# Cross-attention laid into the query projection, weights released by halves, first loads reordered, and the router's first tile moved before the second tile's turn

## The chip, the cores and the metric

One core of one Trainium2 chip. The metric is the device time of one execution in microseconds; for the kernel before it is the median of three runs. The five engines named below are PE (TensorE, matmuls and transposes), DVE (VectorE), ACT (ScalarE), POOL (GpSimd) and SP (which here only issues transfers). Each works through its own list of instructions in order and waits on semaphores.

## What is computed

A two-layer transformer block followed by one mixture-of-experts block, on 256 rows of width 1024 in float32. What the change touches, cut down:

```
# block 1, each of 2 layers: mixer, then cross-attention, then SwiGLU, each followed by a layer norm
q = (u @ cq_w).reshape(B, S, 4, 256)
k, v = split(mem @ ckv_w)
p = softmax(einsum('bshd,bmhd->bhsm', q, k) * 256 ** -0.5)
o = einsum('bhsm,bmhd->bshd', p, v).reshape(B, S, 1024)
cross = o @ co_w
# block 2: after attention and the merge
x = x + g_a * (y @ w_out)
hf = rms(x) * (1 + sc_f) + sh_f
# router: 4 groups of 4 experts, best group, best two experts of it
x = x + g_f * moe(hf)
```

## The kernel before, in words

All weights are streamed once, as units of 1 MB (128 partitions of 2048 floats), in the order that `stream_plan` writes out. A unit lands in one of three raw buffers (five in the expert stage, where two "landing" buffers join). `split_half` turns each half of it (1024 columns) into a high part `whs` by an ACT copy (L207) and a low part `wls` by a DVE subtraction (L211); there are three such split slots, and in the last stage a fourth. Every product is done as three matmuls on those parts (`mm3`, L199). A unit's raw buffer is free for the next transfer when its second half is split; its split slot is free when the last matmul that reads it is done. Up to three units are split ahead. `release` (a unit's last matmul) puts as many splits into the lists of ACT and DVE as there are free slots (`pump`), unless `state["hold"]` or `state["slow"]` is set; with `slow` the splits come one half at a time at each `tick`; `feed(k)` puts in k halves at once. So the splits stand in the same ordered lists as all other work of ACT and DVE.

`gemm_fm` multiplies with the weights as the stationary side (two units, four column tiles of four steps each, two banks) and `gemm_tm` with the activations stationary (two units, two row tiles t). Before the change every matmul of a unit waits for both halves (`split_tok[n]` is a flat list of the two tokens). Both call `tick()` along the way, and a tick advances the first generator in `side`, which is how small chains (transposes, softmaxes) are laid between weight matmuls. `finish_side()` runs what is left.

First loads (L407 on): identity, condition vector, then the two row tiles of x, then the weights, all on SP's list. The two tiles are transposed (`to_fm`, L203), split into high and low parts by ACT and DVE, and the first units are split behind them.

Cross-attention (`cross`): both halves of the query projection `cq_w` run first (`gemm_fm`, four units), and `q_evac` copies each bank out, even ones by ACT, odd ones by DVE (L225). Then `attend` runs with no weight matmuls beside it: `scores(t, hp)` for row tile t and head pair hp (PE; then DVE maximum L222 and scaling L215, ACT exponentials L208, DVE reciprocal L228 and two scalings L215); `turn(hd)` transposes the probabilities of a head (L203; copied out by ACT or DVE); `weigh(hd)` multiplies by the values (L199; high part by ACT, low part by DVE L211). Only then does the output projection `co_w` begin.

The router's surroundings: `w_out_2` is multiplied in two column halves; `merge_evac` adds to the residual h and, with the second half, normalises a row tile (the reciprocal root by POOL, L231). In the middle of the last matmul group `f_fm(0, True)` transposes row tile 0, with all eight modulations on ACT. Behind the projection come, in this order: the low parts of tile 0 (DVE), `f_fm(1)` (transposes of tile 1, modulations, high and low parts), the table `count`, `feed(2)`, `router(0)` (24 small matmuls, logits copied by ACT), `turn_rows(0)` (16 transposes, four ACT copies), `router(1)`. A chain of small DVE operations then chooses experts and places (`first`, `second` are places of a row's two copies), the flag is written, all engines read it and branch, and in the branch `gather` builds the one-hot matrices `Pall` on DVE and multiplies the rows by them (32 matmuls, each bank's four in a row). The expert stage follows.

## Time and profile before

| what | value |
|---|---|
| median of three runs | 1680.62 us (1676.35 to 1683.83) |
| the profiled execution | 1681.34 us |
| its span in the profile | 1679.4 us |
| PE busy in the span | 1596.6 us (95%) |
| DVE, ACT, POOL busy | 1151.0, 903.9, 79.7 us |

The profile is of one execution. A row of its timeline gives the start, the duration, engine, line of the kernel, operation, written tile <- read tiles, shape, count, and in brackets how long the engine had been idle and what released it. The span is 1.94 us shorter than the time of that execution; sums are made against 1681.34.

### The profile page before, as it was taken

To read this page: it belongs to the slowest core of one execution; us is meant where nothing else is said; L and a number is where in the kernel's file an instruction comes from. 1 tells how busy PE (TensorE), PEld (TensorE's weight loads), DVE (VectorE), ACT (ScalarE), POOL (GpSimd) and SP (SyncE) were. 2 spreads that over 40 slices of the span, in tenths; PEclk is the share of its full clock that TensorE was granted. 3 is DMA by queue.
4 is the path that set the end of the run, shared out by engine and by line. 5 is a ranking of instruction groups with operands and counts; after the bars stand their busy time and mean duration, and the time that the engine had idled before them with its cause. 6 is when DMAs were issued, how large, how long until landed. Compare 5 with 4: busy or idle time off the path is not lost.

```text
span 1679.4 us, 20455 instructions
## 1 busy us (share of the span) xinstructions
PE 1596.6 (95%) x8036; PEld 1303.4 (78%) x8036; DVE 1151.0 (69%) x1617; ACT 903.9 (54%) x1377; POOL 79.7 (5%) x75
## 2 busy tenths in 40 slices
PE   7999999989999999989999899999989969999997
PEld 7987788776888789878878667888767758777786
DVE  7457655657545584667566478866664669999997
ACT  5466443435444364764434254544353448888885
POOL 0010000001000000100000000000200000000005
PEclk9999999999999999999999999999999879999999
DMA  7445234535654454542356278874440318999995
GB/s 286 177 153 198 89 112 158 194 126 211 242 198 177 149 202 175 204 172 86 116 200 226 75 259 296 315 257 175 150 169 26 119 63 302 364 374 369 370 371 177
DMA packets 52202, 339.35 MB, mean 202 GB/s; under 512 B 7835, under 2 KB 8477, under 8 KB 13316
## 3 DMA queue, kind: packets, MB, share of 16 engines
q1 hardware_dynamic: 48932, 331.79, 53.7%
q0 software_dynamic: 3168, 6.20, 1.0%
q8 instruction: 65, 1.06, 0.3%
q14 instruction: 37, 0.30, 0.1%
HBM read 332.82 MB, written 10.49 MB: 204 GB/s over the span
## 4 chain that ended last, share of the span: by engine, by line
PE 70%; DVE 15%; ACT 8%; DMA 3%; issue 3%; POOL 1%; ACTq 0%; DVEq 0%; SPq 0%
PE bank L199 66%; DVE wls L211 6%; PE bank L203 4%; ACT whs L207 3%; DMA raw<-in_ws_dram 3%; ACT arena L208 1%; DVE arena L211 1%; DVE sm L222 1%; ACT P1h L1847 1%; DVE h L211 1%; DVE arena L219 1%; POOL sm L231 1%; DVE arena L844 1%; ACT arena L207 1%; DVE arena L215 1%
## 5 line engine op out<-in xcount | busy, mean ns | idle before, releaser
L211 DVE TENSOR_TENSOR wls<-raw,whs 128x1024 fp32r<-128x1024 f32 x442 | 523.5, 1227 | 243.4 <-ACT whs L207 242.8
L207 ACT ACTIVATE whs<-raw 128x1024 fp32r<-128x1024 f32 x442 | 443.2, 1051 | 276.1 <-PE bank L199 193.3
L199 PE MATMUL bank<-whs,P1h 128*128 128x512 f32 (+1 forms) x732 | 291.2, 398 | 5.2 <-DVE P1l L1849 2.0
L199 PE MATMUL bank<-whs,P1l 128*128 128x512 f32 (+1 forms) x732 | 285.5, 390 | 0.0
L199 PE MATMUL bank<-wls,P1h 128*128 128x512 f32 (+1 forms) x732 | 285.1, 390 | 0.0
L199 PE MATMUL bank<-whs,P0h 128*128 128x512 f32 (+1 forms) x640 | 257.6, 402 | 6.3 <-DVE P0l L211 2.5
L199 PE MATMUL bank<-whs,P0l 128*128 128x512 f32 (+1 forms) x640 | 250.2, 391 | 0.0
L199 PE MATMUL bank<-wls,P0h 128*128 128x512 f32 (+1 forms) x640 | 250.1, 391 | 0.0
L199 PEld LDWEIGHTS bank<-whs,P1h 128*128 128x128 f32 x732 | 138.4, 189 | 36.2 <-DVE P1l L211 3.6
L199 PEld LDWEIGHTS bank<-whs,P1l 128*128 128x128 f32 x732 | 138.3, 189 | 29.2
L199 PEld LDWEIGHTS bank<-wls,P1h 128*128 128x128 f32 x732 | 138.4, 189 | 26.9
L199 PEld LDWEIGHTS bank<-whs,P0h 128*128 128x128 f32 x640 | 122.1, 191 | 40.3 <-issue 6.7
L199 PEld LDWEIGHTS bank<-whs,P0l 128*128 128x128 f32 x640 | 121.7, 190 | 25.8
L199 PEld LDWEIGHTS bank<-wls,P0h 128*128 128x128 f32 x640 | 122.0, 191 | 23.9 <-issue 0.7
L207 ACT ACTIVATE arena<-bank 128x256 f32<-128x256 f32 (+1 forms) x131 | 59.8, 463 | 82.6 <-PE bank L199 67.6
L208 ACT ACTIVATE arena<-arena,sm 128x128 f32<-128x128 f32 (+2 forms) x80 | 40.1, 502 | 92.7 <-DVE sm L215 92.7
L203 PE MATMUL bank<-ident,arena 128*128 128x128 f32 x386 | 64.6, 287 | 19.9 <-DVE arena L225 8.7
L199 PE MATMUL bank<-P0h,whs 128*128 128x256 f32 x256 | 74.3, 290 | 4.1 <-DVE wls L211 4.1
L231 POOL TENSOR_TENSOR sm<-sm,mhalf 128x1 f32<-128x1 f32 (+1 forms) x30 | 24.3, 811 | 1089.8 <-DVE sm L215 952.4
L203 PEld LDWEIGHTS bank<-ident,arena 128*128 128x128 f32 x386 | 49.9, 151 | 31.8 <-ACT arena L207 8.4
L199 PE MATMUL bank<-P1h,whs 128*128 128x256 f32 x256 | 73.7, 288 | 0.0
L199 PE MATMUL bank<-P0h,wls 128*128 128x256 f32 x256 | 73.1, 286 | 0.0
(267 smaller groups left out, 2497.1 us busy)
## 6 DMA issues: line engine op xcount, KB each, us to landing
raw<-in_ws_dram SPq DMA_DIRECT2D x264, 1024.0 KB, 4.9
landing<-in_ws_dram SPq DMA_DIRECT2D x38, 1024.0 KB, 7.1
lnb<-in_ln_g_dram SPq DMA_DIRECT2D x6, 512.0 KB, 5.8
lnb<-in_ln_b_dram SPq DMA_DIRECT2D x6, 512.0 KB, 6.5
ydram<-arena POOLq DMA_DIRECT2D x4, 512.0 KB, 11.8
mid<-in_bias_dram SPq DMA_DIRECT2D x1, 2048.0 KB, 7.6
h<-in_x_dram SPq DMA_DIRECT2D x2, 512.0 KB, 4.0
lnb<-in_mem_dram SPq DMA_DIRECT2D x1, 1024.0 KB, 13.1
```

The costliest lines, as they stand in the source:

```text
L199: return PE.put(lambda e: e.matmul(out, lhsT, rhs, start=start, stop=stop, skip_group_check=skip), w, inc)
L203: return PE.put(lambda e: e.transpose(out, in_, ident[0:n, 0:n]), w, inc)
L207: return AC.put(lambda e: e.activation(out, in_, func, bias=bias, scale=scale), w)
L208: return AC.put(lambda e: e.activation(out, in_, func, bias=bias, scale=scale, accum_out=acc), w)
L211: return VE.put(lambda e: e.tensor_tensor(out, a, b, op), w)
L215: return VE.put(lambda e: e.tensor_scalar(out, a, s1, None, op0), w)
L219: return VE.put(lambda e: e.scalar_tensor_tensor(out, a, s, b, op0, op1), w)
L222: return VE.put(lambda e: e.tensor_reduce(out, a, AX.X, op), w)
L231: return GP.put(lambda e: e.tensor_tensor(out, a, b, op), w)
L844: v3 = VE.put(lambda e, k=k: e.tensor_tensor_scan(xc[:, k, :], ra[:, k, :], gi[:, k, :], 0.0, ALU.mult, ALU.add), [v2])
L1847: a = AC.put(lambda g, hi=hi, at=place_of: g.activation(hi, at(AC), ACT.Copy, bias=0.0, scale=1.0), [[T["all", k] for k in range(k0, k1)], ...
```

## The change

Weights by halves: the token of a unit becomes a pair of lists, and matmuls of the first half of the steps wait for the first half alone. First loads: the first row tile of x goes ahead of identity and condition, the second stays behind them. Cross-attention: `attend` is a side chain of the second half of `cq_w`; scores of heads 0 and 1 at its first two ticks, nothing at the third, and at the fourth (behind the last unit) turns 0 and 1, scores of heads 2 and 3, weighing of heads 0 and 1, turns 2 and 3; heads 2 and 3 are weighed behind the first matmul group of `co_w`. Router: with the mode "low parts later" four of tile 0's modulations go to DVE, its low parts stand in `merge_evac` (the first issued behind POOL's power, the second behind tile 1's normalisation), splits are held until `router(0)` and `f_fm(1)` are issued, then `feed(3)`. Routing: the offsets' cast leaves the placement chain, the one-hot matrices are built ahead of the branch, and the gather runs all banks for row tile 0, then for row tile 1.

```diff
@@ split_half
-                split_tok[n] = [split_tok[n], tok]
+                split_tok[n] = [[split_tok[n]], [tok]]
...
+        def half_of(tok, kk, per):
+
+            return tok[0] if isinstance(tok, list) and 2 * kk < per else tok
...
@@ first loads
+        xr = ins["x"].rearrange("a (t p) d -> p (a t) d", p=128)
+        c_h = [load(h[:, 0, :], xr[:, 0, :], s="d_h0")]
         c_ident = load(ident[:, :], ins["ident"], s="d_ident")
         c_cond = load(sm[:, 640:656], ins["cond"], s="d_cond")
-        xr = ins["x"].rearrange("a (t p) d -> p (a t) d", p=128)
-        c_h = [load(h[:, t, :], xr[:, t, :], s=f"d_h{t}") for t in range(2)]
+        c_h.append(load(h[:, 1, :], xr[:, 1, :], s="d_h1"))
...
@@ to_fm
-                        if i == 0 or early:
+                        if i == 0 or early is True:
...
@@ gemm_tm (and in the same way gemm_fm, mlp, up, down)
-                            part(w, slice(None), kk), first, closes and kk == per - 1, tok,
+                            part(w, slice(None), kk), first, closes and kk == per - 1, half_of(tok, kk, per),
...
@@ cross
-            for c in range(2):
-                gemm_fm("cq_w", P0, N["t"], (2 * c, 2 * c + 1), q_evac(c), by_unit=True)
-            xfree = PE.last()
...
-                for hp in range(2):
-                    for t in range(2):
-                        scores(t, hp)
-                        if t:
-                            yield
+
+                for t in range(2):
+                    scores(t, 0)
+                    yield
+                yield
                 turn(0)
                 turn(1)
+                for t in range(2):
+                    scores(t, 1)
+                for hd in range(2):
+                    weigh(hd)
+                    oT[0].append(X[("o", hd)])
+                turn(2)
+                turn(3)
                 yield
-                for hd in range(2, 6):
-                    weigh(hd - 2)
-                    if hd < 4:
-                        turn(hd)
-                    if hd % 2:
-                        yield
-
+                for hd in range(2, 4):
+                    weigh(hd)
+                    oT[1].append(X[("o", hd)])
+                yield
+
+            oT = [[], []]
+            gemm_fm("cq_w", P0, N["t"], (0, 1), q_evac(0), by_unit=True)
+            finish_side()
             at = attend()
-            next(at)
             side.append(at)
-            finish_side()
+            gemm_fm("cq_w", P0, N["t"], (2, 3), q_evac(1), by_unit=True)
+            assert len(oT[0]) == 2 and not oT[1]
+            xfree = PE.last()
             gb = load_ln(l, 2)
             rs = {}
-            oT = [[X[("o", hd)] for hd in range(2)], [X[("o", hd)] for hd in range(2, 4)]]
             src = [(P1, t, oT) for t in range(2)]
             gemm_tm("co_w", src, lambda i: i, res_evac(rs, 0))
+            assert len(oT[1]) == 2
+            finish_side()
...
@@ merge_evac
                     g = gtt(smv(o + 5, 1), q, mhalf[:, 0:1], ALU.pow, a)
+                    if t:
+                        fT[0][2](0)
                     xn_[t] = ts(xs[:, t, :], h[:, t, :], smv(o + 5, 1), None, ALU.mult, None, g, Q["ph"])
+                    if t:
+                        fT[0][2](1)
+                        state["slow"], state["hold"] = False, True
...
-                        mid=lambda: fT.__setitem__(0, f_fm(0, True)))
+                        mid=lambda: fT.__setitem__(0, f_fm(0, "low parts later")))
...
-        for n in range(2):
-            fT[0][2](n)
-        fT = [fT[0][0], f_fm(1, False)[0]]
-        count = arr(5632, 512)
-        for j in range(4):
-            n_ = ts(count[:, j * 128:(j + 1) * 128], cst[:, 256:384], float(128 * j + 1), None, ALU.add, None, c_cst, Q["ph"])
-        feed(2)
+        fT[0] = fT[0][0]
...
+
         a0 = router(0)
+        fT[1] = f_fm(1, False)[0]
+        state["slow"], state["hold"] = True, False
+        count = arr(5632, 512)
+        for j in range(4):
+            n_ = ts(count[:, j * 128:(j + 1) * 128], cst[:, 256:384], float(128 * j + 1), None, ALU.add, None, c_cst, Q["ph"])
+        feed(3)
         turn_rows(0, (5, 2, 3, 6))
         a1 = router(1)
...
@@ placement
-        v_off = vcopy(offi[:, :], begins, d_)
...
+        p_at = []
+        for t in range(2):
+            p_ = ts(Pall[:, t, :], count, first[:, t:t + 1], None, ALU.is_equal, None, n_, v_place, Q["ph"])
+            p_at.append(stt(Pall[:, t, :], count, second[:, t:t + 1], f32(Pall[:, t, :]), ALU.is_equal, ALU.add, p_))
         v_slot = ts(slot, slot, -1.0, None, ALU.add, None, v, v_place)
+        v_off = vcopy(offi[:, :], begins, v_slot)
...
@@ gather
                 for k in range(8):
-                    for i in range(4):
-                        t, p = i // 2, i % 2
-                        m = mm(banks[k][:, :], rows[p][:, t, k * 128:(k + 1) * 128], Pall[:, t, :], i == 0, i == 3,
-                               p_, rows_tok, bankfree[k], inc=(i == 3))
+                    for p in range(2):
+                        mm(banks[k][:, :], rows[p][:, 0, k * 128:(k + 1) * 128], Pall[:, 0, :], p == 0, False,
+                           p_at[0], rows_tok, bankfree[k])
+                for k in range(8):
+                    for p in range(2):
+                        m = mm(banks[k][:, :], rows[p][:, 1, k * 128:(k + 1) * 128], Pall[:, 1, :], False, p == 1,
+                               p_at[1], inc=(p == 1))
```

## Rows read from the trace of the kernel before

**Rows 1.** The profile's page, part 1: busy time and share of the span, instructions.

```profile
PE 1596.6 (95%) x8036; PEld 1303.4 (78%) x8036; DVE 1151.0 (69%) x1617; ACT 903.9 (54%) x1377; POOL 79.7 (5%) x75
```

**Rows 2.** Busy us by stretch: from:to, length, then each engine, PEclk, DMA share, GB/s.

```profile
344.80:368.24 23.44, 17.65 (x82) 14.32 (x80) 12.53 (x28) 8.85 (x23) 0.00 (x0) 0.93 0.31 123
...
920.57:944.15 23.58, 17.79 (x82) 14.47 (x80) 12.54 (x28) 8.96 (x23) 0.00 (x0) 0.93 0.34 125
...
1455.00:1490.00 35.00, 34.90 (x155) 27.87 (x155) 33.23 (x37) 30.47 (x41) 1.92 (x2) 1.00 0.99 371
```

**Rows 3.** Chain that ended last, first layer's cross-attention: start us, us, what.

```profile
345.99 2.36 DVE wls L211 x2
348.35 0.61 DVE sm L222
...
351.07 0.61 DVE sm L222
...
358.88 3.53 PE bank L199 x8
...
362.85 1.73 PE bank L199 x8
```

**Rows 4.** Waits of PE in the whole span: us in total, times, longest us.

```profile
PE bank L199 <- DVE wls L211: 6.0, 5, 4.1
```

**Rows 5.** Chain that ended last, the first 90 us.

```profile
0.73 0.40 SPq L245
...
1.66 3.44 DMA h<-in_x_dram
...
13.88 72.47 PE bank L199 x504
```

**Rows 6.** Timeline of DVE, first layer's query projection: start us, us, instruction [idle <-releaser].

```profile
336.45 0.69 DVE L225 COPY arena<-bank 128x512 f32<-128x512 f32 x1
```

**Rows 7.** Timeline of ACT in the same stretch, the two splits of co_w's units.

```profile
339.14 2.01 ACT L207 ACTIVATE whs<-raw 128x1024 fp32r<-128x1024 f32 x2 [3.75 <-PE bank L199]
...
344.90 2.00 ACT L207 ACTIVATE whs<-raw 128x1024 fp32r<-128x1024 f32 x2 [2.34 <-PE bank L199]
```

**Rows 8.** Chain that ended last, around the router.

```profile
1352.67 1.14 DVE wls L211
1353.81 1.22 DVE P1l L211 x2
...
1355.15 2.72 PE bank L199 x24
...
1360.10 1.44 PE bank L199 x24
```

**Rows 9.** Timeline of ACT around the router.

```profile
1357.18 1.99 ACT L207 ACTIVATE whs<-landing 128x1024 fp32r<-128x1024 f32 x2
...
1359.23 1.05 ACT L207 ACTIVATE P0h<-bank 128x512 fp32r<-128x512 f32 x2
...
1361.57 0.27 ACT L207 ACTIVATE arena<-bank 20x128 f32<-20x128 f32 x1 [0.33 <-PE bank L199]
```

**Rows 10.** Timeline of POOL, two pairs of powers on one column.

```profile
1000.29 1.07 POOL L231 TENSOR_TENSOR sm<-sm,mhalf 128x1 f32<-128x1 f32 x2 [30.13 <-DVE sm L216]
...
1184.95 2.34 POOL L231 TENSOR_TENSOR sm<-sm,mhalf 128x1 f32<-128x1 f32 x2 [11.44 <-DVE sm L216]
```

**Rows 11.** Chain that ended last, from the placement to the gather.

```profile
1369.89 0.18 DVE sm L215
...
1370.98 0.50 DVE Pall L215
...
1371.51 0.75 DVE Pall L219
...
1373.49 10.25 PE bank L199 x32
```

**Rows 12.** The page, part 6: transfers, KB each, median us from issue to landing.

```profile
raw<-in_ws_dram SPq DMA_DIRECT2D x264, 1024.0 KB, 4.9
```

More of the change, by code:

```diff
@@ L522, in gemm_fm @@
                                 part(x, slice(None), k), k == 0 and ct % 2 == 0, k == 7,
-                                tok, [r[ui] for r in ready] if by_unit else ready, bankfree[b] if k == 0 else None, skip=True,
+                                half_of(tok, kk, 4), [r[ui] for r in ready] if by_unit else ready, bankfree[b] if k == 0 else None, skip=True,
                                 inc=(kk == 3 and ct % 2 == 1))
@@ L1181, in up_chunk @@
                         m = mm3(banks[b][:, :], part(P0, slice(None), k, slice(t * 128, (t + 1) * 128)),
-                                part(w, slice(None), kk), k == 0, k == 7, tok,
+                                part(w, slice(None), kk), k == 0, k == 7, half_of(tok, kk, 4),
                                 ready[t][0] if k < 4 else ready[t], bankfree[b] if k == 0 else None, inc=(kk == 3))
@@ L1218, in down_chunk @@
                                     part(w, slice(None), k, slice(hf * 512, (hf + 1) * 512)), c == 1 and k == 0,
-                                    c == nch and k == 1, tok, done[("hT", c - 1)],
+                                    c == nch and k == 1, half_of(tok, k, 2), done[("hT", c - 1)],
                                     bankfree[b] if c == 1 else None, inc=(k == 1))
@@ L1634, in build @@
         fT = [None, None]
+        fbuf = P1
         def f_fm(t, early):
-            return to_fm(xs[:, t, :], t, range(8), P1, xn_[t], scale=cols[:, 40:48], shift=cols[:, 32:40],
+            return to_fm(xs[:, t, :], t, range(8), fbuf, xn_[t], scale=cols[:, 40:48], shift=cols[:, 32:40],
                          free=[spl_free[used[SPL]], A["cols", 1]], tmp=arr(0, 1024), early=early)
@@ L1765, in build @@
         d_ = tt(begins, ends, cnt, ALU.subtract, d_)
-        v_off = vcopy(offi[:, :], begins, d_)
         v_flag = ts(flag[:, :], cmax, 128.0, None, ALU.is_le, None, v1_)
         place3 = place.rearrange("p (t e) -> p t e", t=2)
-        d_ = tt(place3, mask.rearrange("p (t e) -> p t e", t=2), bcast_mid(begins, 2), ALU.mult, v_off)
+        d_ = tt(place3, mask.rearrange("p (t e) -> p t e", t=2), bcast_mid(begins, 2), ALU.mult, d_)
         d_ = tt(place, place, slot, ALU.add, d_, v)
@@ L1810, in gather @@
                 z = [GP.put(lambda e, x=x: e.memset(x[:, :, 512:640], 0.0), [start]) for x in xall]
-                for t in range(2):
-                    p_ = ts(Pall[:, t, :], count, first[:, t:t + 1], None, ALU.is_equal, None, n_, v_place, start)
-                    p_ = stt(Pall[:, t, :], count, second[:, t:t + 1], f32(Pall[:, t, :]), ALU.is_equal, ALU.add, p_)
                 T["gate"] = gates_()
@@ L1926, in up @@
                         m = mm3(banks[b][:, :], part(x_of(e), slice(None), k), part(w, slice(None), kk),
-                                k == 0, k == 7, tok, T["x", e, ui], bankfree[b] if k == 0 else None, inc=(kk == 3))
+                                k == 0, k == 7, half_of(tok, kk, 4), T["x", e, ui], bankfree[b] if k == 0 else None, inc=(kk == 3))
                     if ui == 0:
@@ L1964, in down @@
                         m = mm3(banks[b][:, :], part(hid, slice(None), 2 * i + k),
-                                part(w, slice(None), k, cols_), i == 0 and k == 0, i == 1 and k == 1, tok,
+                                part(w, slice(None), k, cols_), i == 0 and k == 0, i == 1 and k == 1, half_of(tok, k, 2),
                                 T["hT", c], bankfree[b] if i == 0 and k == 0 else None, inc=(k == 1))
```

## The prediction

> **What bounds the kernel now.** First the page's first part [rows 1]: PE is busy for 95% of the span, so time can only come from the stretches in which it isn't, or in which its clock is low. I then asked where those are. Busy time by stretch [rows 2] shows two alike, one in each layer's cross-attention, from the last matmul of the query projection to the first of the output projection: 23.44 and 23.58 us long, PE busy for 17.65 and 17.79. The row of the expert stage is the contrast: PE 34.90 of 35 us at full clock, DVE 33.2. Nothing that only brings weights sooner can help there; what is gained earlier must simply arrive there earlier.
>
> The chain of waits inside the first of those stretches [rows 3] shows why PE stands. DVE finishes a weight split (345.99 to 348.35) that is queued ahead of the softmax; then each of four score tiles takes one turn of DVE, ACT and DVE, 2.72 us from one maximum to the next (348.35 to 351.07); only then, at 358.88, does weighing begin, and its first group takes 3.53 us where a later one of the same size takes 1.73. The clock had fallen: its mean in the stretch is 0.93.
>
> The list of PE's waits [rows 4] says what weights by halves can give: all waits of PE for a weight's low part come to 6.0 us in five places, 4.1 of them at the start.
>
> **The change, part by part.**
>
> *Start.* The first tile of x is issued at 1.66 and lands 3.44 later; it would take the identity's place at 0.73 [rows 5], 0.93 earlier. The first matmul at 13.88 [rows 5] stands at the end of a chain of transposes, ACT copies and weight splits with no transfer's wait in between. With halves it needs one half less, 1.18 (two halves take 2.36 [rows 3]). Together 2.1. Lower end 1.2: if the first weights land too late, only the half counts. Upper end 2.5. The 72 us of matmuls behind it are gapless, so it stays gained. The identity and the condition are issued 0.46 later each; both are small and ready before the tile.
>
> *Halves elsewhere.* The other four waits are 6.0 - 4.1 = 1.9 us, each shorter than a half. They lie in stretches where other chains end soon after, so I take 1.0, between 0 and 1.9. Each half brings its own wait into PE's list, but the list had two waits per unit already.
>
> *Cross-attention.* Inside the second half of the projection PE gets two score groups, some 1.75 us each by the weighing group of equal size (1.73 [rows 3]), and it waits some 0.3 for head 1's query, which DVE copies at 336.45 to 337.14 [rows 6] behind a split. So the projection ends 3.9 later. From its end DVE sets the pace, since its list is in order: the split of the output projection's third unit, released by that end, is done 3.55 after it (348.35 - 344.80 [rows 2, 3]); the second transposed copy, 0.65; the two remaining score tiles, 2 x 2.72; the low parts of heads 0 and 1, 1.2 (a pair takes 1.22 [rows 8]). That is 10.85, and 0.2 for PE to start. PE fills it with transposes, scores and two weighings and waits twice, together under 2 us, so its clock stays up. The other two weighings stand inside the output projection's first pass, 2 x 1.73. Sum 3.9 + 10.85 + 0.2 + 3.5 = 18.4 against 23.4: 5.0 gained. The second layer's stretch is its twin, so 10.0 in all. The upper end is all of the idle time (5.8) and of the slow clock (3.5 - 1.7), 7.6 a layer; the lower end is 2.5 a layer, if every link waits for half of a split more. At the third tick nothing is issued; the splits of the projection's last units lie in ACT's and DVE's lists between the score chains, and both chains are done before the last tick by my count. The layer norm's two loads are issued behind the transfers that wait for those splits, as before, and nothing needs them until the norm.
>
> *Router.* Tile 0's low parts no longer stand behind half a weight split and tile 1's normalisation (1352.67, 1353.81 [rows 8]); the second is done at 1353.4. One of them now runs while POOL computes tile 1's power. Two such powers took 1.07 us at 1000.29 and 2.34 at 1184.95 [rows 10]: in the first DVE subtracted out of a PSUM bank, in the second it subtracted one SBUF tile from another for 1.22 us, as it would here for 0.6. So I add 0.6, and `router(0)` starts at 1354.0. The Trainium skill, "SBUF — State Buffer", section "Who interferes with whom", says that a VectorE instruction with two SBUF inputs and a GpSimd instruction that reads SBUF keep each other out for the whole instruction. By that rule the 0.6 is due; by the row at 1000.29 alone it would be 0, and the sum 0.6 better; the row at 1184.95 agrees with the rule.
>
> `router(0)` takes 2.7 [rows 8]. Tile 1's transposes, which filled PE's wait from 1352.7, come behind it, at 1356.7: 4.0 later. ACT and DVE had then been some 0.5 late for them, waiting for the buffers of tile 0's low parts, so tile 1's high parts end 3.5 later. Behind these in ACT's list stand the fed splits, now three halves in place of two at 1357.18 [rows 9], 1.0 more, then four copies at 1359.23, then tile 1's logits at 1361.57, before which ACT idled 0.33. So the logits come 3.5 + 1.0 - 0.3 = 4.2 later. PE's `router(1)`, at 1360.10 [rows 8], would be ready about a microsecond later than before and isn't the limit. The whole chain of routing follows the logits.
>
> Against it: the first one-hot tile starts without the 1.09 us of slot and branch (1369.89 to 1370.98 [rows 11]), 0.2 sooner for the cast, and PE needs only the first (0.50 + 0.75) to start; the second's 1.2 lie under the first pass. Gain 1.1 + 0.2 + 1.2 = 2.5. The gather's 10.25 [rows 11], half of it at the low clock, stay; PE has been idle as long in front of it. Net for router and routing: 4.2 - 2.5 = 1.7 lost; between 2.5 gained (the fed splits aren't in the way) and 4 lost.
>
> **Sum:** 2.1 + 1.0 + 10.0 - 1.7 = 11.4. The profiled execution took 1681.34, of which the span is 1679.4; 1681.34 - 11.4 = 1669.9. The median shown, 1680.62, is 0.7 lower, which I don't resolve: 1670.
>
> **The rivals.**
>
> *The block in the cross-attention gives half.* PE, DVE and ACT are all in order, so each link can wait for a split that stands ahead of it. For it: in the stretch DVE works 12.5 us even now [rows 2]. Against it: splits are at most two in the new stretch. Gain 2.5 a layer: 1681.3 - 6.4 = 1675, no change that counts.
>
> *The router's part is free.* If the three fed halves slip into ACT's idle time, 4.2 is not lost and 2.5 stays: 1681.3 - 15.6 = 1665.7. For it: PE's own order delays `router(1)` little. Against it: ACT is already within 0.33 us of the limit there [rows 9].
>
> *Weights by halves do nothing* (both halves come due together): 1.2 less at the start, 1.0 less elsewhere, 1672.1.
>
> *Slower: transfers.* The splits of the output projection's first and third unit now stand in ACT's and DVE's lists ahead of the softmax. If their transfers were late, the softmax would wait with them; a transfer takes 4.9 [rows 12]. Two units, two layers: 19.6, so 1669.9 + 19.6 = 1689.5. It breaks even at 11.4 / 4 = 2.9 us per unit. Against it: at 339.14 and 344.90 [rows 7] these splits waited for PE, not for a transfer, and now they are due later.
>
> **How the numbers follow.** No change is what lies within 0.5%, 8.4 us of 1680.6. Chances: forecast 0.48, half in the cross-attention 0.20, router free 0.17, halves nothing 0.08, transfers 0.05, something else 0.02. The forecast, the free router and half of the third case lie below 1672.2, less a part of the forecast's own spread: 0.62 faster. Slower 0.05, the rest 0.33. The range runs from the free router with some of the cross-attention's upper end (1663) to half in the cross-attention with the start's lower end and a microsecond beside it (1677).
>
> **What would show it.** First matmul near 11.8. Between the projections of cross-attention some 11 us of lists with PE waits under 2 us in one place, clock 1.0, and the output projection's first matmul some 8 us sooner after the start of the query projection's second half than now, of which 3.5 go back into the weighings behind it. `router(0)` ahead of tile 1's transposes at low clock, ACT's logits copy behind three split halves, 4 us later after the last matmul of the projection than now; the gather's first matmul right behind the first one-hot tile. Wrong would be: ACT waiting for transfers inside the cross-attention, PE idle more than 3 us in one place there, or the logits no later than before.

## The result, and the profile after

The changed kernel took 1661.41 us (median of 4 executions, 1660.68 to 1664.62) against 1678.81 for the kernel before (4 executions), a ratio of 0.9896 with a 95% interval of 0.9868 to 0.9925. Run once more beside 17 executions of before it took 1664.86 (6 executions) against 1675.63, ratio 0.9923 (0.9906 to 0.9941). So it is faster by 0.8 to 1.0 per cent, 13 to 17 us where 11.4 were predicted; the range began at 1663. Over this study before ran 96 times with a mean of 1677.7, the changed kernel 10 times with a mean of 1663.3. One execution of `halves_ffn` took 5512.52 us; it is left out of every figure here.

The profiled execution took 1662.02, its span is 1660.1. The page's first part, which answers to [rows 1]:

```profile
PE 1590.9 (96%) x8036; PEld 1304.0 (79%) x8036; DVE 1151.3 (69%) x1621; ACT 901.5 (54%) x1373; POOL 80.7 (5%) x75
```

PE has 5.7 us less to be busy with, although it executes the same 8036 matmuls: a busy PE includes the time at the low clock, at which matmuls take longer (further below, ten of them 3.78 us in place of 2.16).

Since most matmuls stand in the same order in every kernel of this study, the profiles can be cut at the same matmul. The table gives the start of the first layer's query projection, the length of each stretch after it, and the start of the last matmul, in us. (The row "before" is the execution that the prediction read; "again" is a second profile of the same kernel.)

| profile | query proj. starts | cross 1 | to cross 2 | cross 2 | feed-fwd 2 | attention, w_out | router, routing | gather | experts | last matmul |
|---|---|---|---|---|---|---|---|---|---|---|
| before | 321.21 | 66.97 | 508.92 | 68.06 | 206.96 | 157.88 | 43.49 | 12.22 | 286.26 | 1671.98 |
| before, again | 320.99 | 67.02 | 508.92 | 67.99 | 205.25 | 152.87 | 43.47 | 12.25 | 286.23 | 1664.99 |
| after | 321.28 | 61.61 | 507.18 | 64.31 | 203.07 | 155.97 | 44.50 | 11.92 | 282.80 | 1652.64 |
| after, again | 319.22 | 63.29 | 510.06 | 64.38 | 204.22 | 155.05 | 44.47 | 11.84 | 283.09 | 1655.62 |
| halves_only | 320.35 | 67.05 | 508.64 | 68.09 | 202.57 | 156.07 | 43.32 | 12.16 | 284.29 | 1662.53 |
| cross_only | 321.36 | 61.70 | 508.85 | 62.72 | 204.81 | 154.31 | 43.35 | 12.14 | 286.18 | 1655.42 |
| router_only | 321.39 | 67.12 | 510.34 | 67.93 | 204.95 | 156.83 | 44.28 | 11.60 | 284.47 | 1668.92 |
| after_no_halves | 320.52 | 63.26 | 510.09 | 66.72 | 205.47 | 157.69 | 44.41 | 12.09 | 284.59 | 1664.85 |
| old_loads | 319.76 | 61.67 | 511.77 | 62.67 | 202.47 | 153.53 | 44.49 | 11.88 | 283.22 | 1651.46 |
| feed_first | 319.29 | 63.21 | 511.62 | 62.71 | 202.45 | 153.41 | 42.62 | 12.80 | 284.32 | 1652.43 |
| turns_first | 319.23 | 61.65 | 511.76 | 62.95 | 202.95 | 156.13 | 41.07 | 11.94 | 285.01 | 1652.70 |
| cross_halves | 320.28 | 63.28 | 511.64 | 62.85 | 204.94 | 157.31 | 43.44 | 12.22 | 284.63 | 1660.59 |
| one_wait | 323.33 | 66.99 | 508.62 | 67.97 | 205.03 | 156.91 | 43.43 | 12.21 | 284.30 | 1668.80 |

Read it by columns. *Cross 1* has three values and no others: 67.0 without the reordering, 61.6 or 63.3 with it. The feed-forward takes 202.4 to 204.9 with all halves and 204.8 to 207.0 without any. The experts take 286.2, 284.4 or 283, with one exception. The stretch of attention and w_out wanders between 153 and 158 whatever the kernel. The stretch *to cross 2* wanders too: it is 508.6 to 511.8 in every row but that of the changed kernel's first profile, whose 507.18 is the shortest. PE is busy there for 497.9 us in the shortest and for 501.0 in the longest, at a granted clock of 1.00 and 0.99, so some of what one profile gains or loses is the clock's.

**Cross-attention.** The whole stretches of cross 1 and cross 2, busy time by stretch, first of the kernel before and then of the changed one (columns as in [rows 2]; the number before "0.43" and its like is PEclk):

```profile
321.21:388.18 66.97, 61.18 (x364) 54.25 (x363) 39.36 (x58) 25.08 (x41) 0.43 (x1) 0.97 0.43 157
897.10:965.16 68.06, 62.06 (x367) 54.67 (x365) 40.35 (x60) 24.94 (x41) 0.55 (x1) 0.97 0.46 170
```

```profile
321.28:382.89 61.61, 59.50 (x364) 53.39 (x363) 39.15 (x58) 24.84 (x41) 0.45 (x1) 1.00 0.47 171
890.07:954.38 64.31, 61.80 (x366) 54.81 (x365) 40.15 (x60) 24.61 (x41) 0.55 (x1) 0.97 0.49 180
```

The same stretch of the changed kernel's second profile:

```profile
319.22:382.51 63.29, 61.09 (x363) 54.55 (x363) 39.16 (x58) 24.84 (x41) 0.48 (x1) 0.97 0.46 166
```

DVE and ACT work as long in both profiles; 63.29 differs from 61.61 by 1.68 us, of which 1.59 are PE's busy time, and the mean granted clock says why: 1.00 in one, 0.97 in the other. The two values of the table are one schedule at full clock (2.4 GHz) throughout and with a piece at 1.2.

PE's list of waits between 338 and 366 us of the changed kernel, which was the prediction's "under 2 us":

```profile
PE bank L203 <- DVE arena L215: 1.6, 1, 1.6
PE bank L199 <- DVE P0l L211: 0.4, 1, 0.4
```

And the chain that ended last there, where the split stands ahead of the score tiles exactly as predicted:

```profile
349.85 2.36 DVE wls L211 x2
352.21 0.60 DVE arena L225
352.81 0.61 DVE sm L222
...
355.51 0.61 DVE sm L222
...
358.22 1.21 DVE P0l L211 x2
...
359.56 2.55 PE bank L199 x10
```

The turn of DVE, ACT and DVE is 2.70 (352.81 to 355.51), as in [rows 3], and the output projection's first matmul at 359.56 comes 8.68 before that of [rows 2] (368.24).

**Router.** The timeline of ACT, the three fed halves (answers to [rows 9]):

```profile
1343.70 1.04 ACT L207 ACTIVATE whs<-raw 128x1024 fp32r<-128x1024 f32 x1
1344.64 1.99 ACT L207 ACTIVATE whs<-landing 128x1024 fp32r<-128x1024 f32 x2
1346.54 1.06 ACT L207 ACTIVATE P0h<-bank 128x512 fp32r<-128x512 f32 x2
1347.49 1.08 ACT L207 ACTIVATE P0l<-bank 128x512 fp32r<-128x512 f32 x2
1348.45 0.25 ACT L207 ACTIVATE arena<-bank 20x128 f32<-20x128 f32 x1
```

and of PE, what waits for that last copy:

```profile
1348.75 0.29 PE L203 MATMUL bank<-ident,arena 20*128 20x20 f32 x1 [2.32 <-ACT arena L207]
...
1357.92 0.80 PE L199 MATMUL bank<-Pall,P0h 128*128 128x512 f32 x1 [3.22 <-DVE Pall L219]
```

The list is the predicted one, link by link. From the projection's last matmul to the counting matmuls behind the logits it is 22.0 us in place of 18.5, so 3.5 later; from there to the gather 4.51 in place of 6.99, so 2.48 gained, where the prediction had 2.5. Up to here the net is 1.0 lost. But then come two stretches that the prediction took as unchanged: the gather and the first matmuls of the experts. First before, then after:

```profile
1373.49:1385.72 12.23, 10.24 (x33) 7.85 (x33) 6.51 (x23) 4.17 (x7) 0.00 (x0) 0.77 0.01 1
1385.72:1389.50 3.78, 3.78 (x10) 2.97 (x11) 3.75 (x5) 2.41 (x4) 0.00 (x0) 0.55 0.00 0
```

```profile
1357.92:1369.84 11.92, 9.61 (x33) 7.42 (x33) 8.01 (x27) 4.17 (x7) 0.98 (x2) 0.82 0.00 0
1369.84:1372.00 2.16, 2.16 (x10) 1.81 (x11) 2.16 (x3) 2.16 (x4) 0.00 (x0) 1.00 0.03 8
```

Ten matmuls take 3.78 us at a granted 0.55 and 2.16 at 1.00. That is 1.6 us which the changed kernel doesn't lose.

POOL's power beside the low part of tile 0:

```profile
1334.75 0.93 POOL L231 TENSOR_TENSOR sm<-sm,mhalf 128x1 f32<-128x1 f32 x1 [6.28 <-DVE sm L215]
```

The same power took 0.55 in the kernel before, with nothing on DVE beside it; so 0.38 of the 0.6 came due. (DVE's subtraction had begun 0.16 before the power and had 0.52 to go.) The rule of the Trainium skill ("SBUF — State Buffer", "Who interferes with whom") agrees with the trace in kind.

### The profile page after: what moved, and what is told of

Read it like the earlier page. It is cut to its first block, busy times and chain, and to the rows that moved or that the text cites. A ratio compares the mean times of both kernels' runs of the same rounds, so it can differ in the third digit from the quotient of the medians.

```text
span 1660.1 us, 20347 instructions
## 1 busy us (share of the span) xinstructions
PE 1590.9 (96%) x8036; PEld 1304.0 (79%) x8036; DVE 1151.3 (69%) x1621; ACT 901.5 (54%) x1373; POOL 80.7 (5%) x75
## 4 chain that ended last, share of the span: by engine, by line
PE 72%; DVE 17%; ACT 6%; DMA 2%; issue 2%; POOL 1%; SPq 0%; DVEq 0%; ACTq 0%
PE bank L199 68%; DVE wls L211 7%; PE bank L203 4%; ACT whs L207 2%; DMA raw<-in_ws_dram 2%; DVE h L211 1%; DVE arena L211 1%; ACT arena L208 1%; DVE sm L222 1%; POOL sm L231 1%; DVE arena L219 1%; DVE arena L849 1%; DVE arena L215 0%; ACT arena L207 0%; DVE P0l L211 0%
## 5 line engine op out<-in xcount | busy, mean ns | idle before, releaser
L203 PEld LDWEIGHTS bank<-ident,arena 128*128 128x128 f32 x386 | 48.7, 149 | 32.3 <-ACT arena L207 10.8
L199 PE MATMUL bank<-P0l,whs 128*128 128x256 f32 x256 | 73.6, 287 | 0.0
```

The costliest lines, as they stand in the source:

```text
L199: return PE.put(lambda e: e.matmul(out, lhsT, rhs, start=start, stop=stop, skip_group_check=skip), w, inc)
L203: return PE.put(lambda e: e.transpose(out, in_, ident[0:n, 0:n]), w, inc)
```

## The experiments

Two theories stood at the outset. Theory one: the halves take off waits all over the kernel. Theory two: the gain outside the three rebuilt places is transfers and chance of one profiled execution. Each kernel below changes one thing; ratios are against before, with 95% intervals.

### The parts by themselves

`halves_only`: the kernel before with the hunks of `split_half`, `half_of` and every use of it.

> The kernel before with the weights by halves alone. Theory one (the halves shorten waits of PE all over the kernel that stand in no list because each is under 0.2 us or has another name): 5 to 7 us faster, ratio 0.996 to 0.997, with each expert of the expert stage 0.16 us shorter (ten such steps between 1433 and 1607 of the profiled pair), both mixers some 0.7 us shorter. Theory two (the gain outside the three rebuilt places is slow transfers of the one profiled execution of before): under 2 us, the expert stage as long as before per expert, and in the second layer's feed-forward no less waiting than the transfers give. The prediction: 2.2 us, half of it at the start.

Measured 1672.42 (8 executions) against 1677.9: 0.9971 (0.9960 to 0.9982). Five us as theory one had it. The query projection starts 0.86 sooner, the feed-forward of layer 2 is 2.7 to 4.4 shorter than in the two profiles of before, the experts 1.9; the mixers' 0.7 did not come. So theory one has the time; whether it has the reason is the question of the next section.

`cross_only`: the kernel before with the hunks of `cross`.

> The kernel before with the reordered cross-attention alone. Prediction: 10.0 us faster, 5.0 in each layer, nothing elsewhere. The profiled pair says 5.4 in the first layer and 3.7 in the second, so 9.1, ratio 0.9946. Theory two adds that the second layer's feed-forward, 3.9 us shorter in the changed kernel, is as it comes with the transfers: it may be short or long here; theory one: as long as before, since nothing here touches it.

Measured 1669.88 (11 executions): 0.9961 (0.9951 to 0.9972). In its profile 5.27 and 5.3 us, above the 5.0 predicted for each layer; in the time 6.5 (4.7 to 8.2), below the 10.0 predicted for both. The executions spread from 1664.53 to 1675.03, and the profile is of the fastest of them, so it doesn't show what the others lack.

`router_only`: the kernel before with `merge_evac`, the order around `router(0)` and the routing.

> The kernel before with the router's first tile moved and the routing rearranged, and nothing else. Prediction: 1.7 us slower (4.2 lost before the logits, 2.5 gained behind them). The profiled pair says 3.5 lost and 3.1 gained up to the expert stage, 0.4 slower; and if the low clock at the expert stage's first matmuls (eight of them 0.43 apart in place of 0.23) belongs to this part, 1.6 gained behind it, so 1.2 faster. Either is within 0.1 per cent of no change.

Measured 1677.84 (12 executions): 1.0001 (0.9989 to 1.0012). No change, as each reading had it, so the time doesn't decide between 1.7 us lost and 0.9 gained; in the profile router +0.8, gather -0.6, experts -1.8.

`after_no_halves`: the changed kernel, with

```diff
-            return tok[0] if isinstance(tok, list) and 2 * kk < per else tok
+            return tok
```

in effect.

> The changed kernel with the weights by halves taken out, everything else left. Theory one: 5 to 7 us slower than the changed kernel, so 1667 to 1669, each expert 0.16 us longer again, first matmul back at 13. Theory two: within 2 us of the changed kernel apart from the start, the expert stage's length per expert unchanged.

Measured 1669.24 (6 executions): 0.9949 (0.9934 to 0.9965), so 7.8 slower than the changed kernel's first median and 4.4 slower than its second. Its feed-forward and experts are as long as without halves. In its profile cross 2 is 2.4 us longer than in the changed kernel, and ACT's timeline there shows the prediction's last rival at work:

```profile
903.77 2.01 ACT L207 ACTIVATE whs<-raw 128x1024 fp32r<-128x1024 f32 x2 [0.84 <-DMA raw<-in_ws_dram]
```

A weight is late, the splits behind it are late, and the first score tile waits 2.9 us for DVE (0.3 in the changed kernel):

```profile
PE bank L199 <- DVE arena L225: 2.9, 1, 2.9
```

That execution took 1674.22, the slowest of its six. So the rival is real, at some 2.5 us in place of its 19.6, and seen in one execution.

### Where the halves act

> The kernel before with the halves in the expert stage alone. The traces say ten steps of 0.16, so 1.6 us faster, ratio 0.999, and the stage's first matmuls still at the low clock. If the halves act through late transfers only, which this stage has none of, 0. The prediction had 0.

The halves in `up` and `down` alone: 1677.1 (12 executions), 1.0002 (0.9990 to 1.0014). In the profile the experts take 284.27, 2.0 us less where 1.6 were expected; in the time they are lost in the spread.

> The kernel before with the halves in the two feed-forwards and nowhere else. In the profiles without halves PE waits 6.0 to 6.7 us in the second layer's feed-forward (8.2 in the one of before, 1.9 of it in one place that no other profile has), with them 3.6 to 4.3; the first layer's waits are 3.2 in all of them. So 2 us faster than before, of the 5 that all halves give; the runs' spread, 8 us for before and 3 us with all halves, gets narrower if late transfers of this stage make it.

The halves in `mlp` alone: 1676.92 (11 executions), 0.9993 (0.9979 to 1.0007). Its feed-forward takes 203.9.

> The kernel before with the halves in the projections alone (mixers, attention, cross-attention), not in the feed-forwards nor the experts. All halves gave 4.9 us, the feed-forwards 1.2 and the experts none that their spread shows. If the parts add up, the projections give 3 to 4, ratio 0.998, of which the start has 0.9 to 1.5, and the runs lie closer together than those of before. By the waits in the profiles it is 1 to 2: the feed-forward has 2.3 of them and the experts 1.7.

The halves in `gemm_fm` and `gemm_tm` alone: 1677.29 (12 executions), 0.9997 (0.9984 to 1.0009). So no single place holds the five us: the 3 to 4 that were expected here lie outside the interval, which ends at 2.7; the 1 to 2 expected by the waits lie inside it. In the feed-forward PE's list of waits has one wait that goes with the halves. First before, then halves_ffn, then the longest that is left in halves_only:

```profile
PE bank L199 <- DVE arena L211: 1.2, 1, 1.2
```

```profile
PE bank L199 <- DVE arena L211: 0.6, 1, 0.6
```

```profile
PE bank L199 <- DVE P1l L211: 0.5, 1, 0.5
```

The wait on `arena` (0.6 to 1.8 us) is in all eight profiles without the halves or with a part of them, and in none of the nine with all halves. It isn't a wait for a weight: PE waits for a bank that DVE has to empty, and DVE's timeline of the kernel before has the emptying behind two halves of a weight:

```profile
988.52 2.35 DVE L211 TENSOR_TENSOR wls<-raw,whs 128x1024 fp32r<-128x1024 f32 x2
...
990.86 0.75 DVE L211 TENSOR_TENSOR arena<-arena,bank 128x256 f32<-128x256 f32 x2
```

That list is late from its head. ACT's timeline of before has there two splits that follow two transfers, 12.73 and 15.20 us behind the stretch's start at 965.16:

```profile
977.89 2.01 ACT L207 ACTIVATE whs<-raw 128x1024 fp32r<-128x1024 f32 x2 [1.54 <-DMA raw<-in_ws_dram]
980.36 2.01 ACT L207 ACTIVATE whs<-raw 128x1024 fp32r<-128x1024 f32 x2 [0.46 <-DMA raw<-in_ws_dram]
```

With all halves (stretch from 964.12) it is 11.10 and 13.62:

```profile
975.22 1.99 ACT L207 ACTIVATE whs<-raw 128x1024 fp32r<-128x1024 f32 x2
977.74 2.01 ACT L207 ACTIVATE whs<-raw 128x1024 fp32r<-128x1024 f32 x2 [0.53 <-DMA raw<-in_ws_dram]
```

The two transfers are issued at the same distance from the stretch's start in both, but here the first has landed before ACT comes to it. So half a weight isn't what PE gains here; two transfers land sooner. It is so in the other profiles too: the first lands 10.8 to 10.9 us behind the stretch's start in every profile without the wait on `arena`, and 12.1 to 13.2 in seven of the eight with it (in halves_gemm only the second is late). Why they land sooner in these kernels is open. Nor is that wait the whole of the two us: cross_halves is without it and takes 204.94, because PE then waits 2.0 in another place.

One more place is odd: in the expert stage the gain is eleven equal steps of 0.16 us (1.7 in all), at the first matmul of the down projection of eleven of the sixteen experts. `one_wait` is the kernel before with

```diff
-                split_tok[n] = [split_tok[n], tok]
+                split_tok[n] = [tok]
```

> The kernel before, in which a unit's first matmul waits for the second half's low part alone: it comes behind the first half's on the same engine and counter, so nothing starts sooner, and each unit has one wait less in PE's list. If the 0.16 us per expert, which the halves took off a down projection's first matmul, is the cost of one more wait in PE's list at a moment when it has just stopped, it goes here too: 1.6 us in the expert stage, ratio 0.999. If it is the earlier start on the first half, the expert stage keeps its 286.2 us, and its matmul its 0.44.

Measured 1674.7 (12 executions): 0.9981 (0.9966 to 0.9996). The timeline of PE at that matmul, before and then with one wait:

```profile
1449.92 0.39 PE L199 MATMUL bank<-whs,P1l 128*128 128x512 f32 x1
1450.36 0.47 PE L199 MATMUL bank<-whs,Pall 128*128 128x512 f32 x1
```

```profile
1448.58 0.39 PE L199 MATMUL bank<-whs,P1l 128*128 128x512 f32 x1
1448.86 0.47 PE L199 MATMUL bank<-whs,Pall 128*128 128x512 f32 x1
```

0.44 from start to start becomes 0.28 at ten experts, and 1.39 becomes 1.23 at the eleventh; the experts take 284.30, as with halves. Nothing starts on half a weight here. So in the expert stage it isn't the earlier start that gains, it is one wait less in front of that matmul: the halves hand the second wait to a later one. What the wait costs is an instruction. The Trainium skill, "Perfetto Trace Analysis", "Identifying Dependency Chains", says that an instruction waiting on several engines may have semaphore instructions with the further conditions put ahead of it. The trace agrees: before, this matmul has four waits, three for DVE and one for ACT, one of them on its own weight load and the others in two semaphore instructions that start 0.22 and 0.11 us before it, behind DVE's last result. With one wait less there are three, two of them in a single semaphore instruction, and the matmul starts 0.10 us behind that result in place of 0.26. (No semaphore instruction in these traces has more than two conditions.) Where one wait less saves no instruction, it saves no time: at the expert ahead of the eleven three waits become two, with one semaphore instruction in both kernels, and 0.33 stays 0.33.

In time one_wait gives 3.2 us (0.7 to 5.7), although in its profile the query projection starts 2 us late. So most of what the halves give behind the start can come without half a weight; the intervals don't say how much. The wait on `arena` is gone in one_wait too, with the transfers landing early as in the kernels with halves, but its feed-forward takes 205.03, as long as without halves: PE waits 2.1 in another place there. So of what the halves give, only the start is shown to come from half a weight: the first matmul is at 12.92 in halves_only and at 13.78 in one_wait.

### The start, and the spread

> The changed kernel with the first loads in their old order (identity and condition ahead of x). The prediction had 0.93 us for that order: first matmul at 12.7 in place of 11.8. The traces so far say that nothing of it is left at the first layer's cross-attention (321.28 against 320.35 with the halves alone), since the clock rises at the same moment and falls for longer around 185: then 0 to 1 us faster than the changed kernel, 1660.4 to 1661.4, against 0.9 slower by the prediction.

The changed kernel with the hunk of the first loads undone: 1661.48 (5 executions), 0.9918 (0.9903 to 0.9934), the changed kernel's time. So the 0.9 us of the loads' order, which the first matmul shows (12.65 against 11.79), is not seen in the time.

> The changed kernel once more, unaltered: a second profile and more times beside the same executions of before. The query projection of the first layer's cross-attention began at 321.28 in its first profile, and at 319.23 to 319.75 in three kernels that are the same up to there: if the first is the odd one, about 319.3 to 319.8, so 1.5 to 2 us of the 2.1 at the start arrive. If it is 321.3 again, the start's gain is lost on the way. In time 1661.4 as before.

The query projection started at 319.22: the 321.28 of the first profile was the odd one, and of the 2.1 us predicted some 1.5 to 2 arrive as a rule. Where they went in the odd one is the clock. Up to that matmul PE is busy for 302.1 us in the first profile and for 299.9 in the second. Near 185 us both have a granted clock of 0.51, but behind that the first has the low clock once more. The rows below are of both stretches, for the first profile and then for the second; the second row of each goes from one matmul to the same later one:

```profile
184.70:191.60 6.90, 6.46 (x16) 4.63 (x17) 4.21 (x10) 3.22 (x13) 0.00 (x0) 0.51 0.45 154
249.61:253.02 3.41, 3.41 (x10) 2.89 (x11) 1.24 (x2) 0.60 (x1) 0.00 (x0) 0.51 0.14 60
```

```profile
183.80:190.70 6.90, 5.82 (x15) 4.10 (x16) 4.85 (x11) 2.98 (x12) 0.00 (x0) 0.51 0.44 154
249.07:250.96 1.89, 1.89 (x11) 1.63 (x11) 1.10 (x2) 0.60 (x1) 0.00 (x0) 1.00 0.27 113
```

Two other profiles begin the query projection late, halves_gemm at 322.40 and one_wait at 323.33, and PE is busy there for 302.1 and 302.6 us before it; in the other fifteen it is 299.7 to 300.6. The second measured time was 1664.86, not 1661.4.

> The kernel before once more, unaltered, for a second profile. The first took 1681.34, 3.7 us over the mean of the 79 executions since. If the wait of 1.9 us in the second layer's feed-forward, behind a transfer of 8.1 us, was of that execution, it is absent here, and that stage takes 205.0 to 205.8 as in the other profiles without halves, not 207.3.

The kernel before once more took 1674.3, seven us less than the first profiled execution of the same kernel. The feed-forward is at 205.25, as expected, and the wait is 0.4 in place of 1.7. But the length of the transfer ahead of it was not the reason: it took 8.14 us in the first profile and 8.42 in this one. What differs is that it was issued 60.82 us behind the stretch's start there and 58.82 here; why is open.

```profile
1025.98 8.14 DMA raw<-in_ws_dram
```

```profile
1023.74 8.42 DMA raw<-in_ws_dram
```

Five of the seven us are the clock in attention and w_out, first the earlier profile, then this one:

```profile
1172.12:1304.09 131.97, 125.74 (x575) 93.11 (x574) 81.10 (x144) 57.78 (x94) 13.99 (x12) 0.95 0.31 110
1304.09:1330.00 25.91, 23.79 (x120) 19.95 (x120) 14.77 (x37) 12.32 (x27) 2.05 (x4) 0.80 0.18 57
```

```profile
1170.17:1298.07 127.90, 121.32 (x575) 90.22 (x574) 80.96 (x144) 57.60 (x94) 14.01 (x12) 0.99 0.30 113
1298.07:1323.04 24.97, 21.05 (x121) 16.96 (x121) 14.71 (x37) 12.21 (x27) 2.06 (x4) 0.93 0.16 50
```

The same instructions, DVE and ACT equal to 0.2 us, and five us between them, with a mean clock of 0.95 and 0.80 in one and 0.99 and 0.93 in the other.

### Do halves and cross-attention add up?

> The kernel before with the reordered cross-attention and the halves, without the router's and the loads' parts. If the two add up as their own runs say, 4.9 and 6.5: 11.4 us faster, 1666.5. If the halves also take late transfers out of the new cross-attention (in one profile without halves the first score tile of the second layer waited 2.9 us behind a late weight), more: 14 to 16, 1662 to 1664. The router's and the loads' parts would then be worth 1 to 2 us together, against 0.4 in the prediction.

Measured 1667.9 (6 executions): 0.9944 (0.9928 to 0.9960), 9.4 us. Their own runs add up to 11.4, which the interval (6.7 to 12.1) holds. The whole, beside the same executions of before, was at 0.9923, so the loads and the router would be worth some 3.5 us, though the intervals overlap, and neither showed any of it by itself; the prediction had 0.8 lost (0.9 gained by the loads' order, 1.7 lost in the router).

### Whether the router's loss can be had back

`feed_first`: `feed(3)` ahead of `router(0)`. 

> The changed kernel with the three fed split halves moved ahead of the router's first tile, into the 7.2 us in which ACT idles there; PE's order is the same. If the halves ahead of the logits copy set when the routing starts (the prediction's step), the last logits come about 2 us sooner: ACT is then done with the four copies at some 1345.7 and the copy waits for PE's 1346.2, where it began at 1348.45. So 2 us faster than the changed kernel, 1659.4. If PE's own order sets it, nothing changes.

Measured 1662.13 (6 executions): 0.9921 (0.9906 to 0.9936). No gain. The logits' copy did move, as expected; ACT's timeline now shows it waiting for PE, no longer behind the halves:

```profile
1345.56 0.27 ACT L207 ACTIVATE arena<-bank 20x128 f32<-20x128 f32 x1 [0.56 <-PE bank L199]
```

The router's stretch is 1.9 shorter. But the gather and the first experts are where it went:

```profile
1355.32:1368.12 12.80, 10.49 (x33) 8.03 (x33) 8.02 (x27) 4.17 (x7) 0.98 (x2) 0.76 0.00 0
1368.12:1371.90 3.78, 3.78 (x10) 2.96 (x11) 3.78 (x5) 2.31 (x4) 0.00 (x0) 0.55 0.11 17
```

Granted clock 0.76 and 0.55 in place of 0.82 and 1.00: 0.9 and 1.6 us. What was won ahead of a waiting PE was paid back at 1.2 GHz.

`turns_first`: `feed(1)` and `f_fm(1)` ahead of `router(0)`, `feed(2)` behind it.

> The changed kernel with the second tile's transposes ahead of the router's first tile again, one fed half before them and two behind. They start at some 1336.5 in place of 1339.73, so ACT ends the second tile's high parts at 1341.3, the two halves and four copies at 1345.3, and PE is done with the router by 1345: logits 3 us sooner than in the changed kernel, 1658.4, if the order on PE was as costly as the prediction has it; 2 us, as the variant with the three halves in front, if only ACT's list counts.

Measured 1662.14 (6 executions): 0.9913 (0.9895 to 0.9930). The router's stretch falls by 3.4 us, as expected; the experts are 2.2 longer, so a third of it is left, within the spread.

`fillers`: matmuls that nobody reads in PE's waits, of which the first group is

```diff
+        for i in range(20):
+            mm(banks[0][:, :], P0[0][:, i % 8, 0:128], P0[0][:, 2 * (i % 4):2 * (i % 4) + 2, :], True, True,
+               bankfree[0], inc=(i == 19))
         yfree = PE.last()
```

> The changed kernel with matmuls added whose results nobody reads, into three waits of PE: 20 behind the output projection (5.4 us of waiting there), 6 ahead of the logits' transposes (2.3 us), 8 behind the counting of the slots (3.2 us). At 0.23 us each they fit into the waits. If the low clock in the router, the gather and the expert stage's first matmuls follows from these waits, and is why time gained ahead of it doesn't arrive, the router's 2 to 3 us, the gather's 2.0 and what comes behind go: 3 to 5 us faster than the changed kernel, 1656.5 to 1658.5. If the clock falls whatever PE does there, the same time or up to 3 us slower, as far as the added matmuls run at 0.43 and don't fit.

Measured 1662.38 (6 executions): 0.9904 (0.9887 to 0.9922). Busy time from the projection's end to the gather, of the gather, and of the experts' first matmuls:

```profile
1330.03:1355.57 25.54, 19.99 (x136) 16.60 (x135) 18.92 (x63) 12.86 (x25) 0.93 (x1) 0.90 0.22 83
1355.57:1366.30 10.73, 8.42 (x34) 6.53 (x33) 7.83 (x27) 4.17 (x7) 0.99 (x2) 0.91 0.01 2
1366.30:1370.10 3.80, 3.80 (x12) 3.05 (x13) 3.80 (x5) 2.32 (x4) 0.00 (x0) 0.69 0.18 22
```

The clock follows what PE does: 0.90 where the changed kernel had 0.76 in that stretch, 0.91 in place of 0.82 in the gather, which is 1.2 us shorter. But the third group of fillers ran at the low clock, didn't fit its wait and kept the gather 0.8 later, and the experts began at 0.69. So the mechanism is right and the gain of 3 to 5 us did not come.

`fillers_turns`: both, with the old loads.

> The same three groups of matmuls, with the second tile's transposes ahead of the router's first tile (one fed half before, two behind) and the first loads in their old order. With the clock held up, the 3.4 us by which that order shortened the router's stage are no longer given back behind it: 1654 to 1657. If the clock isn't the reason, 1661 as the others.

Measured 1660.3 (6 executions): 0.9892 (0.9874 to 0.9910). Not told apart from the changed kernel's 0.9896 and 0.9923.

## Why the prediction was wrong

The direction and the mechanisms of the large parts were right; the time was 5 to 9 us too long. By its own steps, sizes from the profiles:

- **"Together 2.1"** at the start, **"so it stays gained"**: the first matmul came at 11.79, as predicted to 0.01; in the other profiles with the same start it came at 11.79 to 12.33. Of the five profiles with both the new loads and all halves four begin the first cross-attention at 319.2 to 319.8, those with neither at 321.0 to 321.4, but for one at 323.3. Right but for the one that was looked at first, which lost it again at the low clock. 72 gapless microseconds don't preserve a gain; it met the clock behind them, at 249.6 us.
- **"5.0 gained"** per layer in the cross-attention: 5.3 where the clock stays up, 3.7 where it doesn't, and PE's waits of 1.6 and 0.4 were what the prediction counted. 9 us in the two layers of the first profile, 10.0 predicted. The list was right link by link, but the size isn't confirmed by the time: cross_only gave 6.5, and 10.0 lies above its interval.
- **"4.2 later"** for the logits, **"2.5"** gained in the routing: 3.5 and 2.48. The error is the sentence that the gather, "half of it at the low clock", stays. It gained 0.3, and the experts' first matmuls 1.6, where the granted clock was another (0.82 and 1.00 in place of 0.77 and 0.55). The net in the profile is 0.9 gained in place of 1.7 lost: a sign. The time of router_only (1.0001) can't tell the two apart.
- **"Halves elsewhere ... I take 1.0, between 0 and 1.9."** This is the step that failed. It priced the halves by the waits that PE's list names after a weight [rows 4]. All halves by themselves measured 4.9 (3.0 to 6.7), of which the start is 0.9. The profiles give about 2 us in the second feed-forward, 0.6 to 1.8 of them under the name of a bank that DVE empties late, and 1.7 in the expert stage, in steps of 0.16 that the list doesn't show. **"Nothing that only brings weights sooner can help there"** stands for the experts by its words: what helped was one wait less. But the code shows that too, and the prediction's sentence that each half "brings its own wait" priced none of it.
- **"which I don't resolve"**: the sum was made against 1681.34. The mean of 96 executions of the same kernel is 1677.7. 3.6 us of the miss are that the profiled execution was a long one. Against the second profile of the same kernel it is 7.0 longer, 1.7 of it in the second feed-forward and 5.0 in the clock of attention and w_out. That was not resolvable from three times, but it belonged in the range.

Together: 1670, less 3.6 for the base, less 2.7 for the halves (3.7 in place of 1.0), less 2.6 for the router and what follows, plus 1.0 for the cross-attention, plus 0.3 for the start, is 1662.4. The mean of the ten executions is 1663.3. That the two are so near is partly luck: these sizes are of single profiles, which the clock moves by some us. By the times of the parts alone (4.9 for the halves, 6.5 for the cross-attention, nothing for the router and the loads) 1677.7 becomes 1666.3. So which parts hold the last three us is not shown.

Of the rivals, "the router's part is free" came nearest in time (1665.7), but not by its mechanism: the fed halves did stand in the way. "Transfers" was seen in one execution of after_no_halves, at 2.5 us.

Left open: why two transfers in the second feed-forward land sooner in some kernels than in others; why cross_only gives less in time than in its profile; what of the attention's and w_out's 153 to 158 us belongs to the halves, since the clock moves them by more; and why the clock falls in one execution of the same instructions and not in another.

## What to carry to other kernels

Don't price a change of waits by the rows that carry its name alone: an in-order engine passes a delay on under other names, gaps too short for the list add up over a loop, and the number of waits ahead of an instruction can count by itself, where one more of them takes one more semaphore instruction. Where PE waits often, time gained ahead of a wait is partly paid back at the low clock, so read the granted clock of the stretch behind the place that you shorten. Before summing against one profiled execution, compare it with the other times of the same kernel, and put the difference into the range.

## What the runs showed of the hardware that was not expected

A wait that another wait on the same counter implies cost 0.16 us at one matmul of eleven experts (0.44 in place of 0.28 at ten, 1.39 in place of 1.23 at one), where it took a second semaphore instruction, and nothing where it took none (0.33 in both). The same instructions at the same places took 61.6 or 63.3 us, and 152.9 or 157.9, by the granted clock alone (1.00 or 0.97; 0.99 and 0.93 or 0.95 and 0.80). And matmuls without any use, put into PE's waits, raised the granted clock of the stretch from 0.76 to 0.90.
